# RWKV-7 / Conformer / MoE layer on one core: the triangular block inversion with exchanged head halves, on all four quarters of the TensorE array

## The reference, cut to what matters

```python
def step(S, inp):
    r_t, d_t, k_t, v_t, kk_t, b_t = inp
    sa = jnp.einsum('bhvk,bhk->bhv', S, -kk_t)
    S = S * d_t[:, :, None, :] + sa[..., None] * b_t[:, :, None, :] + v_t[..., None] * k_t[:, :, None, :]
    return S, jnp.einsum('bhvk,bhk->bhv', S, r_t)
```

## Time and profile before

| what | value |
| --- | --- |
| median of 3 runs | 1169.46 us (1165.02 to 1174.09) |
| the profiled execution | 1168.77 us, its span 1167.0 us |
| mean granted TensorE clock | 0.927 of 2.4 GHz |
| TensorE matmul busy | 973.3 us (83%), 7221 records |
| DVE busy | 567.3 us (49%) |
| GpSimd busy | 346.3 us (30%) |
| ACT busy | 213.5 us (18%) |

### The profile page before, as it was taken

The page is one execution under the profiler, slowest core; times in us unless marked ns, Lnnn a source line. Parts: engine busy times, 40 slices in busy tenths (PEclk is TensorE's granted clock), DMA queues, the critical chain, the costliest instruction groups (busy, mean ns, idle before and its releaser), DMA issues. The chain is left out here.

```text
span 1167.0 us, 17723 instructions
## 1 busy us (share of the span) xinstructions
PE 973.3 (83%) x7221; PEld 571.0 (49%) x7221; DVE 567.3 (49%) x1029; ACT 213.5 (18%) x452; POOL 346.3 (30%) x396
## 2 busy tenths in 40 slices
PE   4897899888979988759899878977887788879796
PEld 4676767766766767525743333333333333333231
DVE  2138757874987498794552111111111334333575
ACT  3231114112411231112011111111111101111102
POOL 0037803970495069300101111011102232222330
PEclk9998999999989999979999889889988888889899
DMA  7332253234415416556469999999999999999931
GB/s 244 122 109 82 81 195 113 71 147 146 133 33 187 151 37 218 169 225 237 159 264 386 418 416 415 416 412 403 408 392 404 413 409 373 408 406 406 385 101 39
DMA packets 98812, 295.65 MB, mean 253 GB/s; under 512 B 19571, under 2 KB 50741, under 8 KB 82072
## 3 DMA queue, kind: packets, MB, share of 16 engines
q1 hardware_dynamic: 80535, 254.02, 57.0%
q0 software_dynamic: 18192, 40.46, 9.5%
HBM read 284.12 MB, written 36.30 MB: 275 GB/s over the span
## 5 line engine op out<-in xcount | busy, mean ns | idle before, releaser
L1275 PE MATMUL bank<-big 64*64 64x64 f32 (+7 forms) x6778 | 917.0, 368 | 166.5 <-DMA big<-in_w_up 74.6
L1275 PEld LDWEIGHTS bank<-big 64*64 64x64 f32 (+3 forms) x6778 | 522.1, 154 | 511.7 <-issue 381.0
L1567 ACT ACTIVATE big<-bank 128x512 f32<-128x512 f32 (+11 forms) x292 | 124.3, 449 | 772.6 <-PE bank L1275 456.1
L1075 POOL DMA_INDIRECT big<-xg,big x32 | 32.1, 1003 | 404.7 <-PE bank L561 340.2
L2016 POOL TENSOR_SCALAR big<-big 128x256 f32<-128x256 f32 x120 | 128.1, 1068 | 0.4
L919 DVE TENSOR_TENSOR big<-big,bank 128x256 f32<-128x256 f32 x32 | 13.5, 420 | 235.5 <-ACT big L1567 235.5
L2028 POOL TENSOR_TENSOR big<-big 128x256 f32<-128x256 f32 x120 | 85.7, 714 | 0.3
L1841 DVE SCALAR_TENSOR_TENSOR big<-big 128x256 f32<-128x256 f32 x120 | 70.5, 588 | 3.8
L979 DVE SCALAR_TENSOR_TENSOR big<-big 128x1024 f32<-128x1024 f32 (+1 forms) x48 | 61.4, 1280 | 17.9 <-DMA big<-yrows,big 14.9
L1092 POOL DMA_INDIRECT big<-yrows,big x48 | 50.3, 1048 | 52.9 <-DVE big L979 30.2
L2012 POOL TENSOR_SCALAR big<-big 128x256 f32<-128x256 f32 x4 | 2.4, 596 | 200.8 <-DVE big L1801 200.8
(11 more groups left out here) (166 smaller groups left out, 449.7 us busy)
## 6 DMA issues: line engine op xcount, KB each, us to landing
big<-in_w_gate SPq DMA_DIRECT2D x64, 1024.0 KB, 15.9
big<-in_w_up SPq DMA_DIRECT2D x64, 1024.0 KB, 21.6
big<-in_w_down SPq DMA_DIRECT2D x64, 1024.0 KB, 15.2
big<-in_w_in SPq DMA_DIRECT2D x29, 1024.0 KB, 5.4
yrows<-big POOLq DMA_DIRECT2D x32, 512.0 KB, 6.7
big<-in_w_out SPq DMA_DIRECT2D x2, 2048.0 KB, 11.3
big<-in_x_prompt SPq DMA_DIRECT2D x2, 1024.0 KB, 7.4
big<-in_state_wkv SPq DMA_DIRECT2D x32, 64.0 KB, 2.3
```

Of the source, the lines that this page charges most:

```text
L1075: pool.indirect_dma_start(out=x[0:n, :], out_offset=None, in_=xg, in_offset=bass.IndirectOffsetOnAxis(ap=idxu[0:n, col:col + 1], axis=0), ...
L1275: return nc.tensor.matmul(out_, lhsT=lhsT, rhs=rhs, start=start, stop=stop)
L1567: return nc.scalar.activation(out_, in_, f, **kw)
```

## The change

It has five parts.

1. `heads(..., across=True)` sends partitions 0 to 63 into PSUM partitions 64 to 127 and 64 to 127 into 0 to 63. A is computed so, and T_st therefore holds the two heads exchanged between the partition halves; Y_st and TT_st stay as they were.
2. `y_mm` needs a stationary operand in the exchanged order. A new product into B[1] and a new tile XW (8x64) hold it, with a mask of its own on DVE. The products for A, X1 and XW are interleaved unit by unit and have one `a_mm` less between them.
3. `t_mm` (across, into B[2]) and `tt_mm` (straight, into B[3]) are interleaved unit by unit; `t_mm` counts at the last unit.
4. DVE's order at the start is XW, T_st, X1, TT_st, and X2's two masks move into level 0, behind the mask of Y, in the place of two taps. TensorE waits for XW's mask ahead of `y_mm` and for X2's masks ahead of `tr_samples`.
5. The ring of banks starts again at B[1] in each group (8 uses).

```diff
+        XW = F.take(NU, CH)
...
-            def heads(out_, lhsT, rhs, start=True, stop=True):
-
-                for lo, hi in halves:
-                    ins = mm(out_[lo:hi], lhsT[lo:hi], rhs[lo:hi], start, stop)
+            def heads(out_, lhsT, rhs, start=True, stop=True, across=False):
+
+
+                for i, (lo, hi) in enumerate(halves):
+                    a, b = halves[1 - i] if across else (lo, hi)
+                    ins = mm(out_[a:b], lhsT[lo:hi], rhs[lo:hi], start, stop)
                 return ins
...
-                    return B[(1, 4, 5)[i % 3]]
+                    return B[(1, 4, 5)[i % 8 % 3]]
...
                 for h in range(2):
                     for u in range(4 * h, 4 * h + 4):
+                        heads(B[0][:, CH * u:CH * u + CH], AR[:, u, 0, :], BP[:, u, :], across=True)
                         ins = heads(B[2 + h][:, 128 * (u % 4):128 * (u % 4) + 128], BP[:, u, :], arf[:, u, :])
+                        ins = heads(B[1][:, CH * u:CH * u + CH], BP[:, u, :], AR[:, u, 0, :], across=True)
                     note(ins, 'a_mm')
-                for u in range(NU):
-                    ins = heads(B[0][:, CH * u:CH * u + CH], AR[:, u, 0, :], BP[:, u, :])
-                note(ins, 'a_mm')
...
-                pe.wait_ge(S['lmask_ready'], 4 * (g + 1))
+                pe.wait_ge(S['lmask_ready'], 5 * g + 1)
...
-                    lambda: (tr_units(BP), tr_samples(), tr_conv_state()),
+                    lambda: (tr_units(BP), pe.wait_ge(S['lmask_ready'], 5 * (g + 1)), tr_samples(), tr_conv_state()),
...
-                        ins = heads(B[0][:, CH * u:CH * u + CH], X1[:, u, 0, :], T_st[:, u, :])
+                        ins = heads(B[0][:, CH * u:CH * u + CH], XW[:, u, :], T_st[:, u, :], across=True)
...
-                    if not last:
-                        for u in range(NU):
-                            ins = heads(B[2][:, CH * u:CH * u + CH], TT_st[:, u, :], Y_st[:, u, :])
-                        note(ins, 't_mm')
                     for u in range(NU):
+                        if not last:
+                            ins = heads(B[2][:, CH * u:CH * u + CH], TT_st[:, u, :], Y_st[:, u, :], across=True)
+                            if u == NU - 1:
+                                note(ins, 't_mm')
                         ins = heads(B[3][:, CH * u:CH * u + CH], Y_st[:, u, :], TT_st[:, u, :])
                     note(ins, 'tt_mm')
...
-                for h in range(2):
-                    dve.wait_ge(S['a_mm'], 5 * g + h + 1)
-                    note(v.tensor_tensor(X1[:, 4 * h:4 * h + 4],
-                                         B[2 + h][:, :].rearrange("p (u w n) -> p u w n", u=4, w=2),
-                                         up.unsqueeze(1).broadcast_to([128, 4, 2, CH]), M), 'lmask_ready')
-                dve.wait_ge(S['lmask_ready'], 4 * g + 2)
...
+                def masked(dst, i, h):
+                    note(v.tensor_tensor(dst[:, 4 * h:4 * h + 4],
+                                         B[i + h][:, :].rearrange("p (u w n) -> p u w n", u=4, w=2),
+                                         up.unsqueeze(1).broadcast_to([128, 4, 2, CH]), M), 'lmask_ready')
+
+                dve.wait_ge(S['a_mm'], 4 * g + 2)
+                note(v.tensor_tensor(XW, bank(1), up[:, 0, :].unsqueeze(1).broadcast_to([128, NU, CH]), M),
+                     'lmask_ready')
                 link(v.tensor_tensor(T_st, bank(0), bc('pair_low'), M), chain)
                 link(v.tensor_tensor(T_st, T_st, bc('eye_st'), AD), 't_ready')
+                masked(X1, 2, 0)
+                masked(X1, 2, 1)
+                dve.wait_ge(S['lmask_ready'], 5 * g + 3)
                 link(v.tensor_tensor(TT_st, X1[:, :, 0, :], bc('pair_up'), M), chain)
                 link(v.tensor_tensor(TT_st, TT_st, bc('eye_st'), AD), 'tt_ready')
-                for h in range(2):
-                    dve.wait_ge(S['a_mm'], 5 * g + h + 4)
-                    note(v.tensor_tensor(X2[:, 4 * h:4 * h + 4],
...
                     link(v.tensor_tensor(Y_st, bank(0), bc(f'level{m}'), M), 'y_ready')
-                    some_taps(2)
+                    if i == 0:
+                        for h in range(2):
+                            dve.wait_ge(S['a_mm'], 4 * g + h + 3)
+                            masked(X2, 4, h)
+                    else:
+                        some_taps(2)
```

5 lines of the change are left out of this document (1 added, 4 removed).

## The result

Over 13 runs of each kernel the changed one takes 1174.65 us (1169.82 to 1176.57) and the one before 1169.53 us: a ratio of 1.0044, 95% interval 1.003 to 1.0058. It is half a per cent slower, 5.1 us, where 6.6 us of gain were forecast. In words of the forecast this is "within 1%", but the sign is settled, and the time lies outside the range.

The account below looks back on a forecast made before the run. Bound: the four groups' TensorE-DVE dialogue, whose end starts the expert loads. Terms 5.2 + 3.6 - 1.5 - 0.7 = 6.6 us gained from 1168.77 gave 1162.2; with the median 0.7 higher, 1163; range 1154 to 1173.

Parts of the forecast that it names:

- within 1%: Whole kernel: time between 1157.8 and 1181.2 us, about what can't be told from no change; chance 0.71.
- What the groups lose or gain passes to the end one to one.: From the four groups to the kernel's end: experts start later or earlier as a whole, nothing afterwards absorbs the difference.
- The first term: Start of the levels, all four groups: TensorE reaches `t_mm` earlier, 8.3 us saved at full clock, 5.2 after clock loss.
- The clock in it: Start of the levels: TensorE's clock falls in half of the groups, 1.55 us each, 3.1 lost; bounds 0 and 10.
- One round for T and TT: Levels: four array quarters work at once, TT's update comes earlier; 3.6 us gained, less 1.5 for a longer round.
- k: Levels: length of the round for T and TT over 0.95 us; taken as 1.1, costing 1.5 us; bounds 1.0 and 2.0.
- The slower rival: Levels: quarters sharing rows take turns, T's update 0.95 us later in 16 levels; 1178 us; chance 0.12.
- The two taps: DVE's taps back in `some_taps(CW)`: hidden in groups 0 to 2, 0.7 us lost in group 3; bounds 0 and 1.0.
- The clock rival: Late levels: the clock falls once in each group, costing 7.6 us in all, which leaves 1170 us; chance 0.11.

## Why the prediction was wrong, point by point

The forecast was 6.6 us gained, the table shows 4.9 lost. Of the 11.5 us between them 6.4 are the table's fourth line, which the sum put at nothing, 4.7 are the levels (2.1 forecast to be gained, 2.6 lost) and 2.8 the start (5.2 and 2.4 gained); the end of group 3 came out 2.4 better than the forecast.

**"What the groups lose or gain passes to the end one to one."** Read for the way from group 3's end to the end of the kernel, this held within the scatter: the profiled execution less the end of group 3 is 657.2 to 663.8 us over all sixteen profiled executions, 661.7 before and 662.9 after. What failed is the step that I made with it and did not look at, from the inversion's end to the group's end. Groups 0 and 2 left the inversion 2.1 and 2.5 us ahead of the old pace and did not end ahead of it by more than 0.3, since `w_in` lands 16 to 17 us behind the first store whenever it is asked for behind it. I had the rows for it: TensorE stood 1.01 us for `in_w_in` in group 0 of the kernel before, and 2.17 us in group 1, which says that the chunk loop already ended on a transfer. The fourth line of the table, +6.4 us, is this step; with it alone the forecast of 6.6 us gained comes to nothing. Half of it is waiting (1.1 us more in group 0, 0.2 less in group 1, 2.2 more in group 2), half the clock that falls behind the wait (1.6 us in groups 0 and 1).

**The first term, 8.3 us of the start.** Right in its parts: `y_mm` 2.15 us behind the first mask (forecast 2.3), the second idle stretch 2.86 us on X2's masks (forecast 3.7; y and BP took 1.3 us longer, at half clock). With the start filled and nothing else changed, at a whole clock in groups 1 to 3, the first two lines of the table come to 7.2 us gained, so 8.3 was nearly right for a whole clock. But in the changed kernel they come to 2.4, where 5.2 were forecast. The kernel with late samples shows what the wait for X2 and the samples still cost: without them, at full clock, the step is 7.48 us, against 9.55 with them and fillers. The new order didn't remove the wait for X2's masks, it cut it in two.

**The clock in it, -3.1 us.** Wrong by its size: by the two sums just given it took 4.8 us of the start, and more in the levels behind it. I let it fall in two groups, for the samples and T's product only. It fell in every group, in group 1 both for y and BP (0.54) and again behind (0.55, 0.60), in group 3 for 10.2 us. Filling TensorE's idle time at full clock took T's update of level 0 to 9.55 us behind the mask in groups 1 to 3, from 10.74 to 10.99: 1.2 to 1.4 us a group in this step alone, and another 0.9 and 1.5 in level 1 of groups 1 and 3. I had written the bound down myself, "with the following `y_mm` slow too, 4 x 2.5 = 10 us", and then taken the half of the smaller case. The Trainium skill, "TensorE: Matmul & The Clock Gate", Part 1 on the HAM clock gate, says that idling throttles the clock and that work must be sustained before it comes back. The rows agree in kind: two idle stretches of some 3 us with 3 us of work between them, and the work on both sides at about half clock.

**One round for T and TT.** k came out at 1.0: 64 records in 1.16 us with the tail, where 32 take 0.95 without it. The two updates stand back to back. The slower rival, that the quarters take turns, is refuted by this row; so is, for this case, the rule of the Trainium skill (the same page, section on packing small matmuls) that a weight load overlaps with running matmuls only if the row groups differ, since T's and TT's tiles share theirs. The 3.6 us gained, less the 1.5 for k, show at full clock only: -1.0 and -1.6 in groups 0 and 2 of the table's third line, more than the 0.5 a group of the forecast (in group 2 some 0.5 of it is DVE's taps, 0.57 us each instead of 0.63). In groups 1 and 3 the clock ate it, and the line sums to 2.6 lost. Nor is the interleaving worth anything that can be measured: with T as a block the time is the same.

**The two taps, -0.7 us.** Not lost: the end of group 3 became 1.7 us shorter. These rows of DVE answer to the earlier trace rows:

```profile
495.58 1.01 DVE L1843 SCALAR_TENSOR_TENSOR big<-big 128x256 f32<-128x256 f32 x2
...
498.83 3.55 DVE L1966 RECIPROCAL big<-big 128x544 f32<-128x544 f32 x1
```

The taps are there, 1.0 us from 495.58, but the kernel before had stood 1.75 us at 489.75 for TensorE, which was itself waiting for a small transfer. That wait is gone, and the taps lie in its place.

**The clock rival** (11%, 1170) named the right resource and one of the places, the late levels of a group: group 3 had half clock from level 4 on. It was priced at 7.6 us, and the load's wait wasn't in it. The only rival whose times include 1174.65 is the one with the quarters in turn, and its mechanism is refuted.

## What to carry to other kernels

Follow a gain past the edited code to the next transfer that something waits for: a wait of 1 us on a DMA in the trace of before means that the work ahead of it has no slack to give, and an earlier request is worth nothing when another queue's stores hold the engines. A reordering that splits one idle stretch of TensorE into two is not cheaper by the difference of the idle times; price the matmuls behind each stretch at both levels of the clock, and test with idle-time matmuls before crediting any term. When a step grows, look at the granted clock and at the mean time of each engine's instructions in it: here some steps grew at a whole clock, because DVE's taps did. Where several small changes each measure nothing, the one combination that takes the wait and keeps the clock may be worth more than their sum (here nothing, nothing, and 12 us together).
